# Norm roots by square root and reciprocal, a moved out slab and a moved condition tile, in a three-layer transformer kernel on one core

## The reference

```python
def rms_norm(x, g):
    return x * rsqrt(mean(x * x, -1) + 1e-6) * g

mod = silu(c) @ ada_w[l] + ada_b[l]               # sh1, sc1, g1, sh2, sc2, g2
h = rms_norm(x, norm_mix[l]) * (1 + sc1) + sh1
x = x + g1 * mixer_l(h)                           # ends in  o @ w_out[l]
h = rms_norm(x, norm_ffn[l]) * (1 + sc2) + sh2
x = x + g2 * conv_ffn(h)                          # u = h @ w_up, conv of 3 taps, silu(gate) * val, @ w_down
```

## Time and profile before

| | us |
|---|---|
| median of three runs | 1179.6 |
| the profiled execution | 1180.95 |
| its span in the trace | 1179.1 |
| TensorE busy | 1144.7 |
| VectorE busy | 540.9 |
| ScalarE busy | 251.3 |

### The profile page before, as it was taken

One profiled execution on the slowest core, in us unless ns is written; L12 is line 12 of the kernel. 1 busy time (PEld: TensorE's weight loads), 2 busy tenths in 40 slices (PEclk: granted clock), 3 DMA queues, 4 the chain that ended last, 5 costly groups with the idle time before them and its releaser, 6 DMA issues.

```text
span 1179.1 us, 14172 instructions
## 1 busy us (share of the span) xinstructions
PE 1144.7 (97%) x5841; PEld 982.2 (83%) x5841; DVE 540.9 (46%) x1065; ACT 251.3 (21%) x470; POOL 24.9 (2%) x87
## 2 busy tenths in 40 slices
PE   6999999999999999999999999999999999999997
PEld 4788878888888878888888888888788888888886
DVE  2455635555655547452555565555823231111113
ACT  3322323000000244653300000025423330000001
POOL 1000330000000000000000000000000000000000
PEclk9999999999999999999999999999999999999999
DMA  9999708878868462270887786844431335354430
GB/s 349 289 331 353 250 3 307 315 270 291 303 224 303 133 72 87 92 250 1 306 311 276 267 309 217 313 142 149 131 114 37 125 115 203 112 178 143 144 106 36
DMA packets 154576, 234.55 MB, mean 199 GB/s; under 512 B 8801, under 2 KB 126609, under 8 KB 154513
## 3 DMA queue, kind: packets, MB, share of 16 engines
q1 hardware_dynamic: 154156, 233.54, 58.8%
q10 hardware_dynamic: 357, 0.12, 0.0%
HBM read 232.19 MB, written 1.44 MB: 198 GB/s over the span
## 4 chain that ended last, share of the span: by engine, by line
PE 90%; DVE 5%; ACT 2%; SPq 1%; issue 1%; DMA 1%; DVEq 0%
PE PS L668 47%; PE PS L737 19%; PE PS L691 7%; PE PS L681 4%; PE PS L844 2%; PE PS L1091 1%; DMA ada_slot<-in_ada_w 1%; DVE ada_acc L1577 1%; PE PS L596 1%; SPq L376 1%; PE PS L1165 1%; SPq L367 1%; PE PS L877 1%; DVE work L1874 1%; PE PS L860 1%
## 5 line engine op out<-in xcount | busy, mean ns | idle before, releaser
L668 PE MATMUL PS<-hT,slot 128*128 128x256 f32 x2672 | 591.2, 380 | 3.0 <-ACT hT L1273 1.7
L668 PEld LDWEIGHTS PS<-hT,slot 128*128 128x128 f32 x2672 | 507.3, 190 | 74.0 <-issue 5.5
L737 PE MATMUL PS<-act,slot 128*128 128x256 f32 x1056 | 239.2, 380 | 1.5 <-DVE act L1704 1.5
L737 PEld LDWEIGHTS PS<-act,slot 128*128 128x128 f32 x1056 | 200.1, 190 | 30.9 <-DVE act L1704 2.3
L1675 DVE TENSOR_SCALAR ffn_work<-PS,pcol 128x256 f32<-128x256 f32 x100 | 50.7, 541 | 314.5 <-PE PS L668 314.4
L1308 ACT ACTIVATE ffn_work<-ffn_work 128x256 f32<-128x256 f32 x66 | 27.5, 417 | 611.9 <-DVE ffn_work L1685 611.9
L1577 DVE SCALAR_TENSOR_TENSOR ada_acc<-ada_slot,cond,ada_acc 128x1024 f32<-128x1024 f32 x119 | 152.5, 1281 | 6.2 <-DMA ada_slot<-in_ada_w 1.5
L691 PE MATMUL PS<-oT,slot 128*128 128x256 f32 x384 | 85.1, 381 | 0.3 <-DVE att_work L1899 0.3
L691 PEld LDWEIGHTS PS<-oT,slot 128*128 128x128 f32 x384 | 72.2, 190 | 11.3 <-issue 1.8
L681 PE MATMUL PS<-xg,slot 128*128 128x257 f32 (+1 forms) x256 | 58.5, 382 | 2.4 <-DVE xT L1639 2.4
L681 PEld LDWEIGHTS PS<-xg,slot 128*128 128x128 f32 (+1 forms) x256 | 47.3, 187 | 12.3 <-issue 5.2
(11 more groups left out here) (277 smaller groups left out, 773.7 us busy)
## 6 DMA issues: line engine op xcount, KB each, us to landing
ada_slot<-in_ada_w SPq DMA_DIRECT2D x144, 512.0 KB, 8.0
slot<-in_ffn_w_up SPq DMA_DIRECT2D x44, 1024.0 KB, 11.3
slot<-in_ffn_w_down SPq DMA_DIRECT2D x22, 1024.0 KB, 5.0
slot<-in_w_up SPq DMA_DIRECT2D x22, 1024.0 KB, 5.1
slot<-in_sb_w_in SPq DMA_DIRECT2D x12, 1024.0 KB, 13.3
slot<-in_w_in SPq DMA_DIRECT2D x11, 1024.0 KB, 5.3
slot<-in_w_down SPq DMA_DIRECT2D x11, 1024.0 KB, 4.9
slot<-in_dsa_w_in SPq DMA_DIRECT2D x10, 1024.0 KB, 5.2
```

The costliest lines, as they stand in the source:

```text
L668: last = mm(PS[:, bank, half * T:half * T + T], slot[s][:, k, m * P:(m + 1) * P], x[:, k, :], start=k == 0, stop=k == KC - 1)
L737: last = mm(PS[:, c // 2, (c % 2) * T:(c % 2) * T + T], w[:, j_odd * D + c * P:j_odd * D + (c + 1) * P], act[:, j_odd, :], start=start and ...
```

## The change

It has three parts.

The roots: `norm_root` loads the square root's table ahead of its first wait, computes sqrt(s + eps) into rstd and signals `root_ready`; VectorE's new `inverse_root` waits for it, takes the reciprocal of rstd in place (128x256), and waits for its own `rstd_ready`. In `normalise` it stands behind the wait for the products' unit. The two roots of hgrn do the same, with `square_root` on ScalarE and reciprocals on VectorE: one of 128x256 for the attention, two of 128x512 for the recurrence. The key norm's root stays as it is.

The slab: in layer 0, out slab 3 goes to unit 1, and the condition sums go to unit 2 (`mods(4, 2)`); since these share banks with `up_raw(0)`, TensorE's wait for their reader (`mods_taken`) moves ahead of `up_raw(0)`.

The tile: in the last chunk of the FFNs of layers 0 and 1 the condition tile stands behind the product.

```diff
-OUT_UNITS = ((1, 0, 3, 2), (0, 2, 3, 1), (0, 3, 1, 2))
+OUT_UNITS = ((1, 0, 3, 1), (0, 2, 3, 1), (0, 3, 1, 2))
...
-                up_raw(0)
                 if l == 0:
                     mods_taken()
+                up_raw(0)
...
-            out_projection(0, started=(6, 6, 6), after=lambda: (was_read(1), mods(4, 1)))
+            out_projection(0, started=(6, 6, 6), after=lambda: mods(4, 2))
...
+            def square_root(dst, ps):
+
+                act_e.preload_act_table(ACT.Sqrt)
+                full(2)
+                act_e.activation(dst, ps, ACT.Sqrt, bias=eps_col[:, :]).then_inc(unit_read[2], 1)
...
             def norm_root(bank):
 
+                act_e.preload_act_table(ACT.Sqrt)
                 act_e.wait_ge(part_full, bk("part_full").next())
                 act_e.activation(part_sum[:, :], PS[:, bank, 0:T], ACT.Copy).then_inc(part_ready, 1)
                 act_e.wait_ge(stat_full, bk("stat_full").next())
-                link(act_e.activation(rstd[:, :], PS[:, bank, 0:T], ACT.Ln, bias=eps_col[:, :]))
-                act_e.activation(rstd[:, :], rstd[:, :], ACT.Exp, scale=-0.5).then_inc(rstd_ready, 1)
+                act_e.activation(rstd[:, :], PS[:, bank, 0:T], ACT.Sqrt, bias=eps_col[:, :]).then_inc(root_ready, 1)
...
+            def inverse_root():
+
+                dve.wait_ge(root_ready, bk("root_ready").next())
+                dve.reciprocal(rstd[:, :], rstd[:, :]).then_inc(rstd_ready, 1)
+                dve.wait_ge(rstd_ready, bk("rstd_ready").next())
...
-                        for v, k in mine[:1]:
+                        ahead = 0 if n == 9 and odd else 1
+                        for v, k in mine[:ahead]:
                             ada(l + 1, v, (k,))
                         product(odd)
-                        for v, k in mine[1:]:
+                        for v, k in mine[ahead:]:
                             ada(l + 1, v, (k,))
...
             root()
+            link(dve.reciprocal(rstd[:, :], rstd[:, :]))
             for c in range(4):
                 ins = dve.scalar_tensor_tensor(oT[:, c, :], oT[:, c, :], col("attn_out_g", c), rstd[:, :],
                                                ALU.mult, ALU.mult)
...
             root()
+            for h in range(0, HH, 2):
+                x = sq_flat[:, D + h * T:D + (h + 2) * T]
+                ins = dve.reciprocal(x, x)
+            link(ins)
```

More of the change, by code:

```diff
@@ L219, in build @@
         stat_full = sem("stat_full")
+        root_ready = sem("root_ready")
         rstd_ready = sem("rstd_ready")
@@ L1522, in _ @@
             skip(1)
-            root(rstd[:, :], PS[:, 4, 0:T])
+            square_root(rstd[:, :], PS[:, 4, 0:T])
             skip(0)
@@ L1532, in _ @@
                 .then_inc(unit_read[1], 1)
-            root(sq_flat[:, D:2 * D].rearrange("p (b n) -> p b n", b=2), PS[:, 4:6, :])
+            square_root(sq_flat[:, D:2 * D].rearrange("p (b n) -> p b n", b=2), PS[:, 4:6, :])
             norm_raw(OUT_UNITS[2])
@@ L1616, in root @@
                 dve.wait_ge(unit_read[2], bk("unit_full2").value())
+            def inverse_root():
+                dve.wait_ge(root_ready, bk("root_ready").next())
+                dve.reciprocal(rstd[:, :], rstd[:, :]).then_inc(rstd_ready, 1)
+                dve.wait_ge(rstd_ready, bk("rstd_ready").next())
             def norm(which, chunks=range(KC)):
                 if len(chunks) == KC:
-                    dve.wait_ge(rstd_ready, bk("rstd_ready").next())
+                    inverse_root()
                 for c in chunks:
@@ L1819, in _ @@
                     ins.then_inc(unit_read[0], 1)
-            out_projection(2, after=lambda: mods(0, 4, 1))
+            out_projection(2, after=lambda: mods(0, 4, 2))
             ffn(0)
```

## The result

The changed kernel takes 1184.43 us (median of 20 runs, 1182.46 to 1186.12), the kernel before in the runs beside it 1180.63 us (20 runs, 1179.0 to 1184.77). The ratio is 1.0027, with a 95% interval of 1.0018 to 1.0035: slower by 0.3%, where 0.4% faster was forecast. The time lies in the forecast's range and on the side of rival (1), which gave 1183.4.

What follows compares the result with a forecast made beforehand. TensorE's own work was taken as nine tenths of the chain, so only its waits could be won: -1.24 - 1.45 - 1.68 - 0.5 = -4.87 us, from 1179.6 to 1174.7 us; range 1172.5 to 1186.0.

Steps and rivals of the forecast that it cites:

- rival (1): Reciprocal costs 6.7 ns a column, hgrn's second root decides: slower, 1183.4 us; chance 0.30, a third by a higher price.
- the price of the reciprocal: First step, on VectorE: 128x256 costs about what other operations do, 0.42 us, and 512 columns 0.69.
- R: Time VectorE needs for the reciprocal of 128x256; taken as 0.42 us.
- The other reading: Slope of the reciprocal's rows of 1 and 4 columns: 6.7 ns a column, 1.86 us for 256, 3.57 for 512.
- Slab and tile: TensorE's waits ahead of `up_raw(0)` and behind `act` in two FFNs go: -1.24 and -1.45 us.
- Mixer norms: Two TensorE waits of 0.84 us behind the shifted hT go, for reciprocals up to 0.8 us: -1.68 us.
- First norm: oT starts 0.17 us later, within TensorE's 0.38 us of slack: 0.
- FFN norms: Reciprocal lengthens VectorE's chain to `act` by about 0.5 us against about 1.8 us of slack: 0, three times.
- Hgrn's attention root: Scaling comes about 1.25 us sooner, the last merge starts near 903.7 instead of 904.20: -0.5 us.
- Hgrn's second root: Two reciprocals of 0.69 us replace 2.4 of load and exponential; TensorE ran without a stop: 0.
- Rival (2): Shorter TensorE idle before 904 to 911 spares the lower clock's 1.7 us: 1173.0 us; chance 0.08.
- Rival (3): Roots bring nothing, as filler functions need their own table or another wait takes over: 1176.9 us; chance 0.05.

Runs made afterwards that it cites:

- e5_sizes: Kernel before plus unread scratch reciprocals and TENSOR_SCALARs of 1 to 512 columns on idle VectorE in the last layer's FFN; one execution, 1182.15 us.
- e1_slab_tile: Kernel before with the slab and the tile moved, roots as they were; ratio to before 0.9965, 1176.01 us.
- e10_mixers: e1_slab_tile with square root and reciprocal in the two mixer norms alone; ratio to before 0.9965.
- e6_one_set: e1_slab_tile with one table set for logarithm and exponential loaded ahead of the roots' wait; ratio to before 0.9925, 1171.61 us.
- e12_first: Kernel before with square root and reciprocal in the first norm alone; ratio to before 0.9999.
- e4_first_hgrn_back: Changed kernel with hgrn's second root and the first norm back to logarithm and exponential; ratio to before 0.9976.
- e3_hgrn_back: Changed kernel with hgrn's second root alone back to logarithm and exponential; ratio to before 0.9991.
- e11_hgrn: Kernel before with square root and reciprocals in hgrn's second root alone; ratio to before 1.0042, 5.0 us slower.
- e8_tile: Kernel before with the two condition tiles alone moved behind the product; ratio to before 0.9975, 2.9 us less.

## Why the prediction was wrong

**The step that failed is the first, the price of the reciprocal.** It set R = 0.42 us, because the reciprocal's rows of 1 and 4 columns lay 4 and 8 ns from TENSOR_SCALAR's. R is 1.75 us. e5_sizes shows what was amiss: at these sizes an operation of 6.25 ns a column can't be told from a cheap one. The other reading, 6.7 ns a column from the operation's own two rows, gave 1.86 and 3.57 us, within 0.25 us of the truth (1.75, 3.32), but that was luck. The same step on TENSOR_SCALAR's two rows gives 5.3 ns for an operation of 0.51, and on the reciprocal's two rows in e5_sizes 4.7 ns, or 1.35 us for 256 columns. The Trainium skill's "VectorE: DVE Perf Modes", section "First, the fixed hardware budget", with its iterative divide and repeat count of 8, pointed the right way. Read as eight cycles a column it was too dear: the runs show 6.25 ns, which at the page's 0.96 GHz would be six.

**Slab and tile: right.** The waits of 1.24 and 2 x 0.73 us went; the timelines of e1_slab_tile and of the changed kernel have none in their place. Measured 4.1 us rather than 2.7; in the profiled executions the surplus is the clock's.

**Mixer norms: wrong by R alone.** For 0.8 us or less the two waits were to go; at 1.75 they went from 0.84 to 0.90. e10_mixers and e6_one_set show both sides: no loss with the reciprocal, and the waits gone once the logarithm is followed by 0.42 us of exponential alone. The cover of the table load held: the copy of the partial sums held nobody up.

**First norm: wrong by R.** It was put at nothing, for an oT 0.17 us later. With R = 1.75, oT comes 1.5 us later by the same working and TensorE's wait there is 3.8 us. By the traces that costs 0.6 us (e12_first) to 1.5 (changed kernel against e4_first_hgrn_back), by how the start went; e12_first's time doesn't show it.

**FFN norms: right for R = 0.42, and at 1.75 short by a little.** The slack was 189.94 - 188.16 = 1.78 us, against 1.75 + 0.05 and the hand-over behind `act`. In layer 0 of the changed kernel `act` is ready at 191.30, just ahead of TensorE's start:

```profile
190.88 0.42 DVE L1717 TENSOR_TENSOR act<-ffn_work 128x256 f32<-128x256 f32 x1
...
191.44 3.69 PE L738 MATMUL PS<-act,slot 128*128 128x256 f32 x16
```

The matmuls ahead of it (174.37 before, 175.79 now) start 1.42 us later than before and those behind it 1.57: 0.15 us are lost here, and 0.2 in layer 1, about what rival (1) had for them.

**Hgrn's attention root: wrong by R.** No gain; the last merge's wait is still 1.9 us.

**Hgrn's second root: wrong by R, and decisive.** The forecast put it at nothing; its slack was 0.2 us plus the 2.4 us removed. Rival (1) put `mixed_ready` 4.5 us past the need from R = 3.57; with 3.32 it was 3.9, and e3_hgrn_back and e11_hgrn measured 4.3 and 5.0.

**The sum in the traces.** From before to the changed kernel TensorE is 2.8 us late behind the first norm (1.3 of it the start), gains 1.4 with the slab and 0.7 to 0.8 with each tile, loses 0.15 and 0.2 in the FFNs and 0.1 in the mixers, and 3.9 at hgrn's second root: 4.3, as the spans grew from 1179.1 to 1183.4.

**The rivals.** Rival (1) is what happened: 1183.4 forecast, 1184.43 measured, and its place was named rightly. Its chance of 0.30 against 0.57 was the mistake. That its time came within 1 us is in part luck, as its price per column was. Rival (2)'s clock stretch came and went in 1.7 us steps, but in kernels whose idle had not changed (e8_tile), so its condition was wrong. Rival (3) fell: no filler function took a table load of its own.

## What to carry to other kernels

An operation's price per element can't be read from rows of one or four elements: there the fixed part is all that is seen. Where such a row is all there is, the change's sign should be worked out for both prices, and the place with the most elements and the least slack looked at first; here that was one root of 1024 columns with 2.6 us of room. And before a function is exchanged for another to save a table load, see whether one set holds both: that won what this change was after, with VectorE left alone.

## What the hardware showed unexpectedly

The reciprocal in fp32 takes 6.25 ns a column and some 150 ns, alike from 16 to 512 columns and in place or not (1753 and 1746 ns for 256), where TENSOR_SCALAR beside it takes 0.51 ns a column. TensorE's granted clock fell to its lower level (1.2 of 2.4 GHz) in stretches that cost 1.7 us each. Kernels with the same work and the same wait of 1.9 us ahead of it had one or had none (0.83 from 902 to 912 before, 1.00 in e8_tile), and profiled executions had from none to five in all. So changes which merely shift the work by 1 to 3 us measured up to 3 us off the sum of their waits.
